# FoX attention: dividing the probabilities on VectorE ahead of their transposes, in place of the outputs behind them

## What is computed

```python
for start in range(0, t, FOX_BLOCK):
    end = start + FOX_BLOCK
    logits = jnp.einsum('bqhd,bkhd->bhqk', q[:, start:end], k[:, :end]).astype(jnp.float32) * scale
    logits = logits + cum_log_f[:, :, start:end, None] - cum_log_f[:, :, None, :end]
    causal = pos[start:end, None] >= pos[None, :end]
    probs = jax.nn.softmax(jnp.where(causal, logits, MASK_VALUE), axis=-1)
    outs.append(jnp.einsum('bhqk,bkhd->bqhd', probs.astype(v.dtype), v[:, :end]))
```

## Time and profile before

| | |
|---|---|
| runs | 1709.38, 1709.78, 1710.87 us |
| the profiled execution | 1708.04 us |
| its span | 1706.3 us |
| TensorE busy | 1641.3 us, 96% |
| VectorE busy | 794.6 us, 47% |
| ScalarE busy | 662.8 us, 39% |
| GpSimd busy | 74.3 us, 4% |
| granted TensorE clock, mean | 0.989 of full |

### The profile page before, as it was taken

How to read it: one execution, slowest core, us unless ns; L and a number is a source line. 1 busy time by engine, 2 the same in 40 slices (tenths; PEclk the granted TensorE clock), 3 DMA queues, 4 the chain that set the end, 5 groups by cost and what they waited for, 6 DMA issues and landing times.

```text
span 1706.3 us, 20672 instructions
## 1 busy us (share of the span) xinstructions
PE 1641.3 (96%) x8070; PEld 1318.6 (77%) x8070; DVE 794.6 (47%) x1315; ACT 662.8 (39%) x1194; POOL 74.3 (4%) x144
## 2 busy tenths in 40 slices
PE   6999999999998989999999999999999999999997
PEld 5888666667775567888888888888888888888886
DVE  5316534436667464533453255555433455555332
ACT  5225127456333463443432143444323334443221
POOL 2000210110102200000000000000000000000000
PEclk9999899999999999999999999999999999999999
DMA  5121000000112244000111133333232433332322
GB/s 151 50 51 38 26 13 25 21 18 30 58 38 87 69 160 155 4 22 1 38 56 38 37 99 99 93 93 93 74 99 89 128 98 118 94 98 93 99 96 96
DMA packets 166921, 121.31 MB, mean 71 GB/s; under 512 B 23448, under 2 KB 140456, under 8 KB 166824
## 3 DMA queue, kind: packets, MB, share of 16 engines
q1 hardware_dynamic: 165496, 115.53, 22.2%
q10 hardware_dynamic: 1328, 4.46, 0.7%
HBM read 115.77 MB, written 4.19 MB: 70 GB/s over the span
## 4 chain that ended last, share of the span: by engine, by line
PE 62%; DVE 1%; ACT 0%; issue 0%; DVEq 0%; ACTq 0%
PE tail_b L100 19%; PE tail_b L101 19%; PE tail_b L102 19%; PE tail_b L2345 2%; PE tail_b L2320 1%; PE tail_b L2309 0%; PE tail_b L2332 0%; PE tail_b L2256 0%; DVE tail_wl L2020 0%; PE tail_b L2380 0%; PE tail_b L2464 0%; DVE tail_xs L2055 0%; ACT tail_xs L1855 0%; DVE XR L2183 0%; PE tail_b L2393 0%
## 5 line engine op out<-in xcount | busy, mean ns | idle before, releaser
L2176 DVE TENSOR_TENSOR ff_wl<-ff_wr,ff_wh 128x512 fp32r<-128x512 f32 (+1 forms) x176 | 168.5, 958 | 329.9 <-ACT ff_wh L1963 329.9
L1963 ACT ACTIVATE ff_wh<-ff_wr 128x512 fp32r<-128x512 f32 (+1 forms) x176 | 148.7, 846 | 377.9 <-PE tail_b L102 377.8
L100 PE MATMUL tail_b<-HH,ff_wh 128*128 128x512 f32 x704 | 273.9, 389 | 0.0
L101 PE MATMUL tail_b<-HL,ff_wh 128*128 128x512 f32 x704 | 273.9, 389 | 0.0
L102 PE MATMUL tail_b<-HH,ff_wl 128*128 128x512 f32 x704 | 273.9, 389 | 0.0
L100 PE MATMUL mix_gb<-HH,mix_wh 128*128 128x512 f32 x432 | 182.5, 422 | 5.4 <-DVE mix_wl L852 5.3
L101 PE MATMUL mix_gb<-HL,mix_wh 128*128 128x512 f32 x432 | 169.9, 393 | 0.0
L102 PE MATMUL mix_gb<-HH,mix_wl 128*128 128x512 f32 x432 | 169.8, 393 | 0.0
L100 PE MATMUL tail_b<-tail_wh,HH 128*128 128x512 f32 x384 | 154.2, 402 | 6.0 <-DVE tail_wl L2020 4.8
L100 PEld LDWEIGHTS tail_b<-HH,ff_wh 128*128 128x128 f32 x704 | 132.2, 188 | 27.7
L102 PEld LDWEIGHTS tail_b<-HH,ff_wl 128*128 128x128 f32 x704 | 132.2, 188 | 27.3
(11 more groups left out here) (347 smaller groups left out, 2444.0 us busy)
## 6 DMA issues: line engine op xcount, KB each, us to landing
ff_wr<-in_ffn_w_up SPq DMA_DIRECT2D x88, 512.0 KB, 3.6
ff_wr<-in_ffn_w_down SPq DMA_DIRECT2D x88, 256.0 KB, 2.7
mix_wr<-in_w_in SPq DMA_DIRECT2D x26, 512.0 KB, 3.4
mix_wr<-in_xa_wkv SPq DMA_DIRECT2D x16, 512.0 KB, 3.6
XR<-in_x SPq DMA_DIRECT2D x8, 512.0 KB, 6.3
XR<-in_x ACTq DMA_DIRECT2D x1, 4096.0 KB, 18.8
tail_wr<-in_xa_wq SPq DMA_DIRECT2D x16, 256.0 KB, 4.0
tail_wr<-in_xa_wo SPq DMA_DIRECT2D x16, 256.0 KB, 3.3
```

Of the source, the lines that this page charges most:

```text
L100: pe.matmul(out, hi_w, hi_x, start=first, stop=False)
L101: pe.matmul(out, hi_w, lo_x, start=False, stop=False)
L1963: act.activation(part(FWH[m % FPART], m), part(FWR[m % FRAW], m), ACT.Copy).then_inc(w_hi, 1)
L2176: dve.tensor_tensor(part(FWL[m % FPART], m), part(FWR[m % FRAW], m), part(FWH[m % FPART], m), ALU.subtract)\
```

## The change

The two matmuls per unit that spread the inverse sums are gone (32 instructions), and so is the copy of their result. `inverse_sums` becomes `normalise`, which after the reciprocal waits for it and multiplies both heads' rows in SC, in place, by the inverse sum of their query: two `tensor_scalar` instructions per unit over (i+1)*128 columns. `fox_out` is a copy. TensorE's transposes wait for these products (semaphore p_norm) where they waited for the exponentials. `normalise(u+1)` stands in iteration u behind maxima(u+2), ahead of the weights' low parts and the other work; `inverse_sums(u+1)` was the first step of iteration u+1.

```diff
-            def inverse_sums(u):
+            def normalise(u):
                 dve.wait_ge(E("expd"), 2 * u + 2)
                 dve.reciprocal(RIN[:, 2 * u:2 * u + 2], SUM[:, 2 * u:2 * u + 2]).then_inc(E("rin"), 1)
+                dve.wait_ge(E("rin"), u + 1)
+                for hh in range(2):
+                    sc = SC[2 * (u % 2) + hh][:, 0:(PAIRS[u][1] + 1) * P]
+                    dve.tensor_scalar(sc, sc, RIN[:, 2 * u + hh:2 * u + hh + 1], None, ALU.mult).then_inc(E("p_norm"), 1)
 
             def fox_out(u):
                 hp, i = PAIRS[u]
                 dve.wait_ge(E("av_mm"), u + 1)
-                dve.tensor_copy(INV[:], M[5][:, P:2 * P]).then_inc(E("inv"), 1)
-                dve.wait_ge(E("inv"), u + 1)
-                dve.tensor_tensor(MX[:, hp, i * P:(i + 1) * P], M[5][:, 0:P], INV[:], ALU.mult).then_inc(E("av_ev"), 1)
+                dve.tensor_copy(MX[:, hp, i * P:(i + 1) * P], M[5][:, 0:P]).then_inc(E("av_ev"), 1)
 
             for u in range(2):
                 logits(u)
                 maxima(u)
+            normalise(0)
             late = range(0)
             for u in range(len(PAIRS)):
-                inverse_sums(u)
                 if u:
                     fox_out(u - 1)
                 if u + 2 < len(PAIRS):
                     logits(u + 2)
                     maxima(u + 2)
+                if u + 1 < len(PAIRS):
+                    normalise(u + 1)
                 for m in late:
                     halves(m, m + 1)
...
-                    pe.wait_ge(E("expd"), 2 * u + hh + 1)
+                    pe.wait_ge(E("p_norm"), 2 * u + hh + 1)
...
-                pe.wait_ge(E("rin"), u + 1)
-                for hh in range(2):
-                    n = 2 * u + hh
-                    pe.matmul(M[5][64 * hh:64 * hh + 64, P:2 * P], RIN[:, n:n + 1].to_broadcast([P, 64]), ident,
-                              start=True, stop=True, skip_group_check=True)
```

## The result

The changed kernel takes 1725.35 us, the median of four runs (1723.24 to 1727.57), beside 1709.58 for the kernel before on the same chip (1705.15 to 1710.87, four runs): 1.0097 times as long, 95% interval 1.0075 to 1.0119. It is slower, by 1%, and 1725.35 lies 0.85 us from the 1724.5 that was predicted.

A forecast was written before the change was run, and what follows sets the result against it. TensorE, busy 96% of the span and in every microsecond of FoX, was taken as the bound. 9.8 us net of steps and savings plus 5.3 for GpSimd's additions made 15.1 longer: 1724.5 us, forecast 1721.5 to 1729 (0.52), range 1717 to 1731.

The forecast's parts named there:

- idle time of TensorE ahead of the transposes: Sign at line 1464, released by line 1062: waits at 13 or so boundaries, about 1.2 us each, none at unit 8.
- the stretch: Sign in FoX: from the first scores to the last outputs, to grow from 117 to about 132 us.
- GpSimd's pairs: Sign at line 458: the pairs of mask additions should stretch from 0.87 to 2 us.
- the wait behind FoX: Sign: TensorE's wait of 2.68 us at 423.50 should shrink to 2.35.
- The steps without GpSimd: Reciprocal and products ahead of transposes at 16 boundaries: 10.4 us later in sum, each with its 0.27 taken off.
- GpSimd's additions: Mask additions beside the products: 0.60 us a unit at 8 boundaries, 0.45 at unit 0, 5.3 us longer.
- The removed matmuls: Spreading matmuls ahead of each unit's outputs: 16 x 0.27 = 4.3 us off TensorE, all on the path.
- The shorter last fox_out: Copy alone at the end of FoX: ScalarE could start 0.33 us sooner, counted once.
- 1, GpSimd without effect: Rival, in FoX: only two-input instructions are held up, the product is not; 9.8 us alone, 1719.6; chance 0.23.
- 2, the clock: Rival, in FoX: waits bring clock drops of 1.2 us or more each; four to eight make 1729 to 1734; chance 0.10.
- 3, the wait hidden: Rival, in FoX: VectorE's chain ends before each unit's outputs, leaving 4.3 + 0.3 us gain, 1705.1; chance 0.05.
- 4, waits won back: Rival, in FoX: VectorE or ScalarE catch up during TensorE's idle time; half recovered, +4 to +6, 1715; chance 0.07.

The follow-up runs named there:

- experiment 1: Changed kernel with GpSimd's mask additions, from unit 3 on, waiting for the products behind the same maxima; 1.0078 times the kernel before, stretch 126.55 us.
- experiment 4: Changed kernel with the removal alone: no products, division left out, transposes waiting for the exponentials; 1.0003 times the kernel before, stretch 113.66 us.
- experiment 8: Changed kernel with exponentials earlier, products ahead of the second piece of logits, GpSimd's additions waiting for products; 1.0005 times the kernel before, stretch 113.81 us.
- experiment 3: Changed kernel with each product over 2 columns only, order and waits kept; 1.0061 times the kernel before, stretch 123.13 us.
- experiment 10: Repeat of experiment 4, the removal alone with the division left out; 0.9995 times the kernel before, stretch 113.74 us.
- experiment 2: Changed kernel with the 32 spreading matmuls put back, result unused, products kept; 1.0079 times the kernel before, stretch 130.38 us.
- experiment 11: The changed kernel run again, unedited; 1.0082 times the kernel before, stretch 129.97 us.
- experiment 9: The kernel before, run again unchanged as an experiment; ratio 1.0003, stretch 116.73 us.

## Why the prediction was right, point by point

**Where.** Most of what was named to show it is there: idle time of TensorE ahead of the transposes at 14 boundaries, 0.9 us each on the mean, released by the products, none at unit 8, granted clock 1.00, the stretch about 130 us for 132. Not there are two signs: GpSimd's pairs grew from 0.87 to 1.25 us at most and not to 2, and the wait behind FoX stayed 2.69 us and did not shrink to 2.35. Shares of busy time said nothing of it: VectorE's is 47% before and after. What told it was the chain at each boundary, from the last scores over the maxima to the product, beside the outputs as its only cover.

**The steps without GpSimd** (10.4 us predicted). Experiment 1 has them nearly alone: 10.1. By unit they agree to 0.05 at 14 of 16; at unit 8 it is -0.21 for -0.27, and only unit 14 is far off, 1.10 for 1.33. There the prediction took the start of the maxima from the trace of before, 395.71, with the 0.25 us that VectorE stood idle ahead of them. In the changed kernel (and in experiment 4) that idle time is not there, and what hangs on the maxima comes some 0.2 us sooner:

```profile
409.47 0.16 DVE L1054 TENSOR_REDUCE mix_nm<-mix_nmx 128x2 f32<-128x6 f32 x1
```

The price of the product, from other lines' rows, holds: 0.68 us a product predicted at 896 columns, and a pair, the second started 0.08 before the first one's end, 1.28 in all; 1.28 measured. The "22 or so us" of added work on VectorE don't follow from this price: it gives 16.5 for the 32 products. They took 15.2 in experiment 8 and 19.1 in the changed kernel, beside the additions. Nothing in the sum hangs on it.

**GpSimd's additions** (5.3 us, 0.60 a unit): right in kind, too large in size. Experiment 1 puts them at 3.4 us, 0.43 a unit where the meeting is full. The nearest row, 0.30 for an instruction of two inputs beside an addition, was doubled for two products. What was measured is about the length of one addition (0.87 / 2) a pair, not two. At 345.06 both engines were done with their pairs at 346.80 (345.09 + 1.71), 1.74 us; at their own lengths, one after another, it would be 0.87 + 1.28 = 2.15, and fully side by side 1.28. The Trainium skill (SBUF — State Buffer, Who interferes with whom) has the second blocked until the first is done. By that, an estimate from the two additions' length, it would have been 0.87 a unit: the trace is with the rule in that there is a hold-up at all, also for a product of one input, and against it in size. The other lengths say more. Where both pairs start together, both engines are done 0.96, 1.07, 1.47, 1.64 and 1.74 us later for products of 128, 256, 640, 768 and 896 columns, and 0.89 for 2 (experiment 3). An estimate from the rows, 0.87 for the additions plus the column part alone of both products, 0.516 ns a column, gives 1.00, 1.13, 1.53, 1.66, 1.79 and 0.87. So it looks as if additions and columns exclude each other, and only the part of a product that is the same at every length (0.218 us) runs beside an addition. It fits the six lengths to 0.06 us, and no experiment of its own tests it.

**The removed matmuls** (4.3 us): alone they give 3.0, by experiments 4 and 10. 0.22 each, and nothing at units 10 and 15, where ScalarE is late. The error was to read what they take from their own start to the next, and not from the instruction ahead to the one behind. Inside the changed kernel they are worth only 0.43 us (experiment 2); at the 14 boundaries with a wait the step was worked out from the chain, where they don't come in, and so the sum is off by this in 0.05 us at unit 8 and as much at the end alone.

**The shorter last fox_out** (0.33 us): nothing. The copy did come alone, but the norm at line 863 was late next, 0.54 us of idle time for 0.18. The prediction's step "a chain over ScalarE and VectorE leads to the wait" left out this second chain.

**The rivals.** 1, GpSimd without effect, falls with experiment 1: 3.4 us. 2, the clock: 1.00 in all of FoX. 3, the wait hidden: it is there 14 times; but experiment 8 shows that another order of the same work does hide it. 4, waits won back: the steps of experiment 1 are those worked out without any recovery, but for the 0.2 us at unit 14.

**How much of the closeness is luck.** By mechanism 15.1 us were predicted (15.4 in the stretch), and 13.2 found. That the forecast meets the median to 0.85 us is luck: in the profiled execution 3.0 us ahead of FoX, where no instruction differs, and 1.6 behind make up for it. In the repeat (experiment 11), beside the same trace of before, it is 1.7 ahead and 3.6 behind, and the whole ratio is 1.0082; beside the repeat of before (experiment 9) the first scores are even 4.3 us earlier and the part behind 6.9 longer. Both intervals, 1.0075 to 1.0119 and 1.0059 to 1.0105, hold the 13.2 us (1.0077).

**What stays open.** In experiments 4, 8 and 10 the stretch is 3 us shorter than before (0.998 of the whole) and the ratios are 1.0003, 1.0005 and 0.9995. Either the 3 us are given back outside FoX, or the variation there hides them. The intervals speak against hiding alone: 0.998 (0.9982 for 3.06 us) lies below those of experiments 4 and 8 and on the edge of that of 10 (0.9982 to 1.0009). The part behind FoX was 1298.5, 1298.2 and 1299.9 us in their profiled executions, and 1297.4 and 1294.2 in two of before: that leans the same way, but a single kernel has spread by 3.2 in it. TensorE's idle time there is 40.2 to 40.4 us for 39.9 and 40.0, so about half a microsecond at most is waiting; the rest would have to be busy time at the lower clock, and no run here shows that an earlier end of FoX brings it.

## What to carry to other kernels

An engine at 47% can still be the one that everything waits for: before work is moved onto it, lay its list beside the waiting engine's at the place of the new wait, and ask what the moved work stands behind that it does not need. Here it was the maxima and, behind those, the exponentials; with both out of the way and GpSimd's additions put off, the same products cost nothing in the stretch. And an instruction taken off the bound engine just ahead of a wait saves next to nothing: 0.43 of 3.0 us was left of it here.

## What the runs showed of the hardware that was not expected

**What a meeting of VectorE and GpSimd costs hardly depends on how much the product reads.** A pair of two-column products took 0.36 us alone and 0.86 beside additions (experiment 3), 0.50 more; a pair of 896 columns 1.28 (experiment 1) and 1.71, 0.43 more. GpSimd's pair was held up by the long products (1.25 us for 0.87) and not by the short ones (0.86).

**The same instructions ahead of FoX take from 292.1 to 298.2 us.** The kernel before itself had its first scores at 292.14 in one profiled execution and at 298.17 in another. The two rows, busy time from the span's start to there:

```profile
0.00:292.14 292.14, 267.86 (x1365) 209.41 (x1365) 122.07 (x166) 117.00 (x197) 29.14 (x70) 0.98 0.21 52
```

```profile
0.00:298.17 298.17, 273.72 (x1365) 212.78 (x1365) 123.07 (x166) 117.11 (x197) 28.07 (x70) 0.97 0.21 51
```

TensorE ran the same 1365 records, stood idle for 24.3 and 24.4 us, and was busy 5.9 us longer, at a granted clock of 0.97 for 0.98: more of the work fell at the level of 1.2 GHz. From 180 to 195 us the granted clock was 0.80 in the first and 0.59 in the second, from 120 to 135 and from 255 to 270 us 1.00 and 0.89 (from 165 to 180 us 0.86 and 0.95, the other way). In all 13 profiled executions of this case the part ahead of FoX lies within these 292.1 to 298.2 us, and no edit touches it. Six microseconds are 0.35% of the kernel, twice what experiments 4 and 8 gained in FoX; an edit of that size is to be judged by the stretch that it touches.
